# Bringing the rows of adaptive modulation into columns: transposes and a VectorE reduce instead of picking products

## The chip, the cores and the metric

The kernel runs on one core of one Trainium2 chip, as one program with one launch. The metric is the device time of the program in microseconds (us). Five engines work side by side, each through its own list of instructions in order, and wait for each other by semaphores: TensorE (PE, with its weight loads PEld), VectorE (DVE), ScalarE (ACT), GpSimd (POOL), and SyncE (SP), which here only issues loads. SBUF is the memory on the chip; PSUM holds TensorE's results, in eight banks of 512 fp32 columns.

## What is computed

Three transformer layers for 256 latent and 256 context tokens of width 1024. The first block has gated DeltaNet, a short convolution and a Fourier mix, and a SwiGLU feed-forward layer; the second block has a layer of retention and mLSTM and a layer of windowed attention, each with its feed-forward layer. Every layer takes its shifts, scales and gates from two condition vectors, one for the latent tokens and one for the context. That part is what the change touches:

```python
mod = jax.nn.silu(c) @ w_mod[layer] + b_mod[layer]
sh1, sc1, g1, sh2, sc2, g2 = jnp.split(mod[:, None, :], 6, axis=-1)
mod_c = jax.nn.silu(c_ctx) @ w_mod[layer] + b_mod[layer]
csh1, csc1, cg1, csh2, csc2, cg2 = jnp.split(mod_c, 6)
...
def modulate(t, gain, shift, scale):
    return rmsnorm(t, gain) * (1 + scale) + shift
```

w_mod is 1024 by 6144 for each of the three layers: 75 MB in fp32 of the 258 MB that the kernel reads.

## The kernel before

Activations lie with features on partitions and tokens on the free dimension. All large products split their fp32 weights in two parts: ScalarE writes wh (line 1517), VectorE or GpSimd writes wl = raw - wh (lines 2037 and 751), and TensorE adds three products (lines 855 to 857, 872 to 874 and 969 to 971). Weights come in 1 MB chunks through three buffers named raw; SyncE issues the next load when the chunk three before it has been used.

The order is a plan written out by hand (`make_plan`): it numbers every PSUM tile in the order in which TensorE fills it. A tile takes the bank of its number modulo eight, so TensorE, at `begin`, waits until the tile eight before it has been read out and freed (`free`, semaphore `bank_free`). `full` waits for a filled tile, `evacuated` for a freed one. `link` is used where an instruction reads what the one before it on its own engine wrote: it adds to the engine's own semaphore and waits for it.

**A modulation chunk** is 256 of the 6144 columns of one layer; there are 24 a layer, 72 in all, numbered 0 to 71. `mod` on TensorE does two things at each call. First the *row* of chunk n (line 906): eight products of 32 columns of condition vectors with 256 columns of weights. The k-th product goes to the 32 partitions of quadrant k % 4, so the result stands in four partial sums: partitions 32j and 32j+1 hold partial j for the latent and for the context vector. The other 30 partitions of a quadrant hold products of neighbouring columns, which nobody uses. ScalarE copies the 128 by 256 result to `modrow` (line 1527, two buffers). Then the *pick* of chunk n - 1 (line 914): `modrow`, 128 columns at a time, is the stationary operand, and the constant `pick`, 128 by 2 with a one in rows 32j of column 0 and rows 32j+1 of column 1, the moving one. That brings features onto partitions and adds the four partial sums: 128 by 2 for each half, 4 columns in the tile `modcol`. VectorE adds the bias and writes `mods` (line 2054), and after chunks 7 and 19 of a layer makes `coef` from the scales (line 2062), which the norms read.

The plan puts nine chunks at the start (the first norm waits for eight of them), six between the first projection's tiles, sixteen into the four steps s of the DeltaNet scan, four around the output projections, and the others into the norms, the feed-forward layers, the retention, the mLSTM and the attention. In the norm stages the order on TensorE is: spread of the reciprocal root (line 946), row, pick, row; ScalarE copies the second row before it writes h_hi (line 1558), and VectorE writes h_lo (line 2095) before TensorE goes on.

In a step of the scan TensorE's order is GR, KK, then row and pick of two chunks, the transpose of a mask product (X0T, line 1098), row and pick, the second X0T, row and pick, and the loop over levels, which begins with line 1112. VectorE takes X0T out of PSUM (line 2280), then does its four chunks in a row (`mod(4)`), then in the last two steps eight operations of line 2290, and then waits for the level loop (line 2328). GpSimd multiplies masks beside it (line 772), with both operands in SBUF. The tile `modcol` of the fourth chunk is eight tiles behind that of the first, so its pick waits until VectorE has finished the first.

Of the kernel before, what the change touches and what calls it, by code (L numbers as in the profile page):

```python
# [30 lines left out]
ALU = mybir.AluOpType  # L31
ACT = mybir.ActivationFunctionType
AX = mybir.AxisListType

P = 128
# [366 lines left out]
def build(nc, dram, out):  # L402
# [26 lines left out]
    modrow = sb("modrow", [P, 2, 256])  # L429
    mods = sb("mods", [P, 3, 48, 2])  # L430
# [17 lines left out]
    def S(name):  # L448
        a, b = SMALL[name]
        return small[:, a:b]  # L450
# [9 lines left out]
    ident = CA("ident")  # L460
# [143 lines left out]
    def bank(*key):  # L604
        return ps[:, tile[key] % BANKS, :]

    def free(ins, *key):
        ins.then_inc(bank_free[tile[key] % BANKS], 1)
# [210 lines left out]
    def _(pe):  # L819
# [74 lines left out]
        def mod_one():  # L894
            n = modn[0]
            modn[0] += 1
            if n == 0:
                pe.wait_ge(sem("cst_ready"), 1)
            if n < MODS:
                w = slot("mod", n)  # L900
                b = begin("modrow", n)

                for k in range(KD):
                    j = k % 4
                    o = SMALL["cvec"][0] + 16 * min(n // 24, 1) + 2 * k
                    ins = nc.tensor.matmul(b[32 * j:32 * j + 32, 0:256], small[:, o:o + 32],  # L906
                                           w[:, 256 * k:256 * k + 256], start=(k < 4), stop=(k >= 4),
                                           skip_group_check=True)
                close(ins)
            if 0 < n <= MODS:  # L910
                evacuated(pe, "modrow", n - 1)
                b = begin("modcol", n - 1)
                for i in range(2):
                    ins = nc.tensor.matmul(b[:, 2 * i:2 * i + 2], modrow[:, (n - 1) % 2, P * i:P * i + P], S("pick"),  # L914
                                           start=True, stop=True)
                close(ins)

        def mod(count=1):
# [97 lines left out]
        m = 0  # L1016
# [11 lines left out]
        b = begin("gt", 0)  # L1028
# [999 lines left out]
    def _(dve):  # L2028
# [14 lines left out]
        def mod(count=1):  # L2043

            for _ in range(count):
                n = modn[0]
                modn[0] += 1
                if 0 < n <= MODS:
# [2 lines left out]
                    lay, c = n // 24, n % 24  # L2051
                    o = 48 * lay + 2 * c
                    bias = S("bmod")[:, o:o + 2].unsqueeze(2).to_broadcast([P, 2, 2])
                    free(V.tensor_tensor(mods[:, lay, 2 * c:2 * c + 2, :],
                                         bank("modcol", n)[:, 0:4].rearrange("p (m v) -> p m v", m=2), bias,
                                         ALU.add), "modcol", n)
                    if c in (7, 19):
                        evacuated(dve, "modcol", n)
# [883 lines left out]
```

## Time and profile before

| | us |
|---|---|
| median of 3 runs | 1952.01 |
| lowest and highest | 1947.19, 1953.04 |
| profiled execution | 1949.81 |
| its span, first to last instruction | 1948.0 |

| engine | busy us | share of the span |
|---|---|---|
| TensorE | 1802.1 | 93% |
| TensorE weight loads | 1553.2 | 80% |
| VectorE | 909.6 | 47% |
| ScalarE | 763.3 | 39% |
| GpSimd | 477.1 | 24% |

The mean granted clock of TensorE was 0.962 of full speed; the clock has two levels, 1.0 (2.4 GHz) and 0.5 (1.2 GHz). A busy share is a mean over stages with different limits, so it says which engine is worth looking at, not what an instruction less is worth. For that the chain of work that ended last is read: it goes back from the last instruction, at each step to what released it.

### The profile page before, as it was taken

The numbers are of one execution on the slowest core, as the hardware profiler recorded it, in microseconds if no ns is written. First come the engines' busy times: TensorE is split into PE (matmuls) and PEld (weight loads), VectorE is DVE, ScalarE is ACT, GpSimd is POOL, SyncE is SP. The second block draws the span as 40 slices with busy tenths as digits, with TensorE's granted clock in tenths as the row PEclk, the third lists the DMA queues.
The fourth block names the chain that finished last, engine by engine and source line by source line (L and its number), as shares of the span: only waits on it lengthen the run. The fifth ranks groups of instructions, "written<-read, shape, count | busy, mean of one in ns | idle before, by whom it ended". The sixth has DMA issues, their size and how long they took to land.

```text
span 1948.0 us, 34252 instructions
## 1 busy us (share of the span) xinstructions
PE 1802.1 (93%) x14608; PEld 1553.2 (80%) x14608; DVE 909.6 (47%) x1659; ACT 763.3 (39%) x1330; POOL 477.1 (24%) x240
## 2 busy tenths in 40 slices
PE   5998998988799999998979789999999989999999
PEld 3777897877789999787778567888888767579998
DVE  1648626565344333535586744222231347744343
ACT  3454532233335564421544324222222344655443
POOL 0135322121113433111233011211212211013443
PEclk8999999999899999899989889999999999999999
DMA  8443244232264544323111123323222337034543
GB/s 316 174 162 130 89 172 153 89 110 88 109 253 163 190 178 168 136 69 127 54 65 66 68 85 130 131 107 130 109 108 103 114 123 274 27 144 162 193 175 129
DMA packets 36581, 261.58 MB, mean 134 GB/s; under 512 B 4048, under 2 KB 4176, under 8 KB 6224
## 3 DMA queue, kind: packets, MB, share of 16 engines
q1 hardware_dynamic: 36432, 259.40, 36.2%
q8 instruction: 117, 1.92, 0.4%
q14 instruction: 32, 0.26, 0.0%
HBM read 258.34 MB, written 1.05 MB: 133 GB/s over the span
## 4 chain that ended last, share of the span: by engine, by line
PE 79%; DVE 11%; ACT 4%; issue 3%; DMA 2%; POOL 1%; SPq 0%; DVEq 0%; ACTq 0%
PE ps L855 19%; PE ps L856 18%; PE ps L857 18%; PE ps L882 2%; PE ps L906 2%; PE ps L969 1%; PE ps L872 1%; PE ps L1124 1%; PE ps L873 1%; PE ps L874 1%; PE ps L970 1%; DVE msq L2492 1%; PE ps L971 1%; PE ps L1112 1%; PE ps L1475 1%
## 5 line engine op out<-in xcount | busy, mean ns | idle before, releaser
L751 POOL TENSOR_TENSOR wl<-raw,wh 128x1024 fp32r<-128x1024 f32 (+1 forms) x179 | 426.5, 2385 | 1241.4 <-ACT wh L1517 1241.4
L855 PE MATMUL ps<-h_hi,wh 128*128 128x256 f32 (+1 forms) x1696 | 556.7, 328 | 5.4 <-POOL wl L751 3.9
L856 PE MATMUL ps<-h_lo,wh 128*128 128x256 f32 (+1 forms) x1696 | 548.9, 324 | 0.0
L857 PE MATMUL ps<-h_hi,wl 128*128 128x256 f32 (+1 forms) x1696 | 548.9, 324 | 0.0
L1517 ACT ACTIVATE wh<-raw 128x1024 fp32r<-128x1024 f32 (+1 forms) x330 | 342.2, 1040 | 402.9 <-PE ps L857 287.5
L855 PEld LDWEIGHTS ps<-h_hi,wh 128*128 128x128 f32 x1696 | 327.8, 193 | 34.3 <-POOL wl L751 7.8
L856 PEld LDWEIGHTS ps<-h_lo,wh 128*128 128x128 f32 x1696 | 327.6, 193 | 25.8 <-issue 2.4
L857 PEld LDWEIGHTS ps<-h_hi,wl 128*128 128x128 f32 x1696 | 327.3, 193 | 23.8
L2037 DVE TENSOR_TENSOR wl<-raw,wh 128x1024 fp32r<-128x1024 f32 (+1 forms) x151 | 187.6, 1242 | 244.3 <-ACT wh L1517 233.1
L855 PE MATMUL ps<-gh,wh 128*128 128x256 f32 (+1 forms) x528 | 169.2, 320 | 0.0
L856 PE MATMUL ps<-gl,wh 128*128 128x256 f32 (+1 forms) x528 | 168.1, 318 | 0.0
L857 PE MATMUL ps<-gh,wl 128*128 128x256 f32 (+1 forms) x528 | 168.1, 318 | 0.0
L2116 DVE TENSOR_TENSOR sil<-ps,sil 128x256 f32<-128x256 f32 (+1 forms) x66 | 33.9, 513 | 258.6 <-PE ps L857 257.2
L855 PEld LDWEIGHTS ps<-gh,wh 128*128 128x128 f32 x528 | 100.5, 190 | 8.7 <-issue 2.0
L857 PEld LDWEIGHTS ps<-gh,wl 128*128 128x128 f32 x528 | 100.6, 190 | 6.9
L856 PEld LDWEIGHTS ps<-gl,wh 128*128 128x128 f32 x528 | 100.6, 191 | 6.8
L1596 ACT ACTIVATE sil<-ps 128x256 f32<-128x256 f32 (+1 forms) x66 | 30.0, 455 | 162.2 <-PE ps L857 160.5
L906 PE MATMUL ps<-raw,small 128*32 128x256 f32 x1152 | 85.5, 419 | 4.0 <-DMA raw<-in_mod 3.5
L1527 ACT ACTIVATE modrow<-ps 128x256 f32<-128x256 f32 x72 | 26.9, 381 | 125.3 <-PE ps L906 125.2
L914 PEld LDWEIGHTS ps<-small,modrow 128*128 128x128 f32 x288 | 40.3, 202 | 40.4 <-issue 30.1
L772 POOL TENSOR_TENSOR d_Xc<-d_Ac,const 128x256 f32<-128x256 f32 x40 | 31.6, 808 | 155.7 <-DVE d_Ac L2271 132.4
L872 PE MATMUL ps<-wh,h_hi 128*128 128x256 f32 x160 | 49.5, 310 | 17.5 <-POOL wl L751 11.0
(417 smaller groups left out, 2694.3 us busy)
## 6 DMA issues: line engine op xcount, KB each, us to landing
raw<-in_mod SPq DMA_DIRECT2D x72, 1024.0 KB, 5.0
raw<-in_ffn_in SPq DMA_DIRECT2D x66, 1024.0 KB, 4.8
raw<-in_ffn_out SPq DMA_DIRECT2D x24, 1024.0 KB, 4.8
raw<-in_w_in SPq DMA_DIRECT2D x16, 1024.0 KB, 4.8
raw<-in_w_gate SPq DMA_DIRECT2D x12, 1024.0 KB, 4.9
raw<-in_w_ab SPq DMA_DIRECT2D x12, 1024.0 KB, 4.8
raw<-in_ffn_out SPq DMA_DIRECT2D x12, 768.0 KB, 4.3
raw<-in_w_at SPq DMA_DIRECT2D x5, 1024.0 KB, 4.9
```

The lines of the kernel that those rows point to most:

```text
L751: nc.gpsimd.tensor_tensor(wl[e % SPLIT][:, 0:entries[e]["words"]], part(e), wh[e % SPLIT][:, 0:entries[e]["words"]].bitcast(F32), ALU.subt ...
L772: nc.gpsimd.tensor_tensor(Xc[:, d, lv % 2], Ac[:, d], mask.unsqueeze(1).to_broadcast([P, 4, 64]), ALU.mult).then_inc(sem("x_level"), 1)
L855: nc.tensor.matmul(b[:, cols], wh[e % SPLIT][:, w], xh(k), start=(k == 0), stop=False)
L856: nc.tensor.matmul(b[:, cols], wh[e % SPLIT][:, w], xl(k), start=False, stop=False)
L857: ins = nc.tensor.matmul(b[:, cols], wl[e % SPLIT][:, w], xh(k), start=False, stop=(k == nk - 1))
L872: nc.tensor.matmul(b[:, 0:256], h_hi[:, k, tk], wh[e % SPLIT][:, w], start=(k == 0), stop=False)
L882: ins = nc.tensor.matmul(b[:, 0:cols], w(k), rhs(k), start=(k == 0), stop=(k == nk - 1))
L906: ins = nc.tensor.matmul(b[32 * j:32 * j + 32, 0:256], small[:, o:o + 32], w[:, 256 * k:256 * k + 256], start=(k < 4), stop=(k >= 4), skip ...
L914: ins = nc.tensor.matmul(b[:, 2 * i:2 * i + 2], modrow[:, (n - 1) % 2, P * i:P * i + P], S("pick"), start=True, stop=True)
L1517: A(wh[e % SPLIT][:, 0:x["words"]], part(e), ACT.Copy).then_inc(hi_ready, 1)
L2037: V.tensor_tensor(wl[e % SPLIT][:, 0:entries[e]["words"]], part(e), wh[e % SPLIT][:, 0:entries[e]["words"]].bitcast(F32), ALU.subtract).th ...
L2116: free(V.tensor_tensor(sil[:, j % 4, c0:T], bank("fb" + nm, j)[:, c0:T], sil[:, j % 4, c0:T], ALU.mult), "fb" + nm, j)
```

## The change

The pick of a chunk becomes two transposes: `modrow`, 128 columns at a time, stays the stationary operand, and the identity is the moving one in transpose mode. The tile `modcol` then holds 256 columns instead of 4: for each half m the four quadrants j of 32 columns, of which the first two (r = 0 and 1) are the partial sums of the two vectors. VectorE's one instruction becomes two: a reduce over j out of PSUM into `mods`, linked, and an addition of the bias on `mods` in place, which frees the tile. Each pick keeps its place on TensorE. In the changed kernel the lines between 914 and 2054 have numbers smaller by one.

```diff
                 evacuated(pe, "modrow", n - 1)
                 b = begin("modcol", n - 1)
                 for i in range(2):
-                    ins = nc.tensor.matmul(b[:, 2 * i:2 * i + 2], modrow[:, (n - 1) % 2, P * i:P * i + P], S("pick"),
-                                           start=True, stop=True)
+                    ins = nc.tensor.transpose(b[:, P * i:P * i + P], modrow[:, (n - 1) % 2, P * i:P * i + P], ident)
                 close(ins)
...
                     bias = S("bmod")[:, o:o + 2].unsqueeze(2).to_broadcast([P, 2, 2])
-                    free(V.tensor_tensor(mods[:, lay, 2 * c:2 * c + 2, :],
-                                         bank("modcol", n)[:, 0:4].rearrange("p (m v) -> p m v", m=2), bias,
+                    parts = bank("modcol", n)[:, 0:256].rearrange("p (m j r) -> p m r j", m=2, j=4)[:, :, 0:2, :]
+                    link(V.tensor_reduce(mods[:, lay, 2 * c:2 * c + 2, :], parts, AX.X, ALU.add))
+                    free(V.tensor_tensor(mods[:, lay, 2 * c:2 * c + 2, :], mods[:, lay, 2 * c:2 * c + 2, :], bias,
                                          ALU.add), "modcol", n)
                     if c in (7, 19):
                         evacuated(dve, "modcol", n)
```

VectorE in the second step of the scan, before the change; d_TTc is the last work on X0T, d_TTc and d_Tmc behind it belong to the level loop:

```order
209 L2280 TENSOR_TENSOR d_TTc<-const_60,ps 128x256 x2
210 L2054 TENSOR_TENSOR mods<-ps,small 128x4 x2
211 L2062 SCALAR_TENSOR_TENSOR coef<-mods,small 128x16
212 L2054 TENSOR_TENSOR mods<-ps,small 128x4 x2
213 L2328 TENSOR_TENSOR d_TTc<-d_TTc,ps 128x256
```

The same place after it:

```order
237 L2280 TENSOR_TENSOR d_TTc<-const_60,ps 128x256 x2
238 L2054 TENSOR_REDUCE mods<-ps 128x4
239 L2055 TENSOR_TENSOR mods<-mods,small 128x4
240 L2054 TENSOR_REDUCE mods<-ps 128x4
241 L2055 TENSOR_TENSOR mods<-mods,small 128x4
242 L2062 SCALAR_TENSOR_TENSOR coef<-mods,small 128x16
243 L2054 TENSOR_REDUCE mods<-ps 128x4
244 L2055 TENSOR_TENSOR mods<-mods,small 128x4
245 L2054 TENSOR_REDUCE mods<-ps 128x4
246 L2055 TENSOR_TENSOR mods<-mods,small 128x4
247 L2328 TENSOR_TENSOR d_TTc<-d_TTc,ps 128x256
```

Each addition out of PSUM (ps) has become a reduce out of PSUM and an addition with both operands in SBUF (mods and the bias in small). VectorE behind the mLSTM, before the change, where rml is the low half of the output projection's input:

```order
741 L2495 TENSOR_TENSOR mout<-mout,gb 128x512
742 L2054 TENSOR_TENSOR mods<-ps,small 128x4 x2
743 L2641 TENSOR_TENSOR rml<-rout,rmh 128x512 x4
744 L2641 TENSOR_TENSOR rml<-mout,rmh 128x512 x4
745 L2037 TENSOR_TENSOR wl_55<-raw_49,wh_52 128x1024
```

And after it:

```order
809 L2495 TENSOR_TENSOR mout<-mout,gb 128x512
810 L2054 TENSOR_REDUCE mods<-ps 128x4
811 L2055 TENSOR_TENSOR mods<-mods,small 128x4
812 L2054 TENSOR_REDUCE mods<-ps 128x4
813 L2055 TENSOR_TENSOR mods<-mods,small 128x4
814 L2641 TENSOR_TENSOR rml<-rout,rmh 128x512 x4
```

Four instructions stand in front of rml in place of two.

## Rows read from the trace of the kernel before

**Rows 1.** The page's part 4: shares of the chain that ended last, by engine.

```profile
PE 79%; DVE 11%; ACT 4%; issue 3%; DMA 2%; POOL 1%; SPq 0%; DVEq 0%; ACTq 0%
```

**Rows 2.** Lines 914 and 2054 by source: duration ns min/median/max, first and last start, form.

```profile
L914 PE MATMUL ps<-small,modrow x288: 165/251/374, 20.3 to 1770.0; 128*128 128x2 f32 x144
L2054 DVE TENSOR_TENSOR mods<-ps,small x72: 147/154/164, 21.0 to 1770.4; 128x4 f32<-128x4 f32 x72
```

**Rows 3.** Timeline, TensorE, chunk 8: start us, us, engine, line, operation, count.

```profile
62.98 0.61 PE L914 MATMUL ps<-small,modrow 128*128 128x2 f32 x4
63.45 0.48 PE L855 MATMUL ps<-h_hi,wh 128*128 128x512 f32 x1
```

**Rows 4.** Transposes of line 1058: by source, and timeline of TensorE at their end.

```profile
L1058 PE MATMUL ps<-const_all,qk x16: 272/272/273, 227.3 to 230.2; 128*128 128x128 f32 x16
...
230.36 0.60 PE L1058 MATMUL ps<-const_all,vT 128*128 128x128 f32 x4
230.71 0.36 PE L855 MATMUL ps<-h_hi,wh 128*128 128x256 f32 x1
```

**Rows 5.** The chain in order of time (start us, us, what), at chunks.

```profile
63.05 0.54 PE ps L914 x4
...
125.81 0.54 PE ps L914 x4
...
791.07 0.54 PE ps L914 x4
...
1220.41 0.54 PE ps L914 x4
...
1513.33 0.54 PE ps L914 x4
```

**Rows 6.** The chain at chunk 6, and the timeline of transposes at the lower clock.

```profile
38.03 0.94 PE ps L914 x4
...
1657.12 1.97 PE L1475 MATMUL ps<-const_all,sc 128*128 128x128 f32 x8
```

**Rows 7.** Timeline of GpSimd, VectorE and TensorE in the scan's second step.

```profile
363.29 2.33 POOL L772 TENSOR_TENSOR d_Xc<-d_Ac,const 128x256 f32<-128x256 f32 x3 [2.03 <-DVE d_Ac L2271]
...
364.50 0.47 DVE L2062 SCALAR_TENSOR_TENSOR coef<-mods,small 128x16 f32<-128x16 f32 x1
365.00 0.32 DVE L2054 TENSOR_TENSOR mods<-ps,small 128x4 f32<-128x4 f32 x2
...
364.54 0.58 PE L914 MATMUL ps<-small,modrow 128*128 128x2 f32 x4 [0.22 <-DVE mods L2054]
```

**Rows 8.** Lines 2535 and 2062 by source: duration ns min/median/max.

```profile
L2535 DVE TENSOR_TENSOR tiny<-scr,rM x8: 147/149/2399, 1017.2 to 1029.4; 32x1 f32<-32x1 f32 x8
...
L2062 DVE SCALAR_TENSOR_TENSOR coef<-mods,small x6: 174/174/470, 43.8 to 1655.4; 128x16 f32<-128x16 f32 x6
```

**Rows 9.** Timeline of GpSimd and TensorE at the output projection's third tile.

```profile
552.36 2.41 POOL L751 TENSOR_TENSOR wl<-raw,wh 128x1024 fp32r<-128x1024 f32 x1 [30.56 <-ACT wh L1517]
...
555.12 0.28 PE L855 MATMUL ps<-mgh,wh 128*128 128x256 f32 x1
```

**Rows 10.** Timeline at two splits and their use, and the chain at chunks 63 and 67.

```profile
1125.98 0.77 PE L855 MATMUL ps<-rmh,wh 128*128 128x512 f32 x1 [6.72 <-DVE rml L2641]
...
1195.71 1.22 DVE L2037 TENSOR_TENSOR wl<-raw,wh 128x1024 fp32r<-128x1024 f32 x1
...
1197.48 0.39 PE L855 MATMUL ps<-h_hi,wh 128*128 128x512 f32 x1
...
1644.70 0.15 DVE mods L2054
...
1654.34 0.84 PE ps L914 x4
```

**Rows 11.** Windows: length; busy PE, PEld, DVE, ACT, POOL; granted clock; DMA share, GB/s.

```profile
227.30:230.70 3.40, 3.40 (x33) 3.40 (x32) 0.00 (x0) 3.15 (x7) 0.00 (x0) 1.00 0.00 0
26.30:43.30 17.00, 15.70 (x107) 9.00 (x108) 0.70 (x5) 2.01 (x6) 0.00 (x0) 0.50 0.93 367
```

## The prediction, made before the changed kernel ran

> **What bounds the kernel now.** Read the chain of work that ended last first: TensorE holds 79% of the span, VectorE 11% [rows 1]. So a TensorE instruction taken out pays only where the chain passes through it. Next read the two lines that the change replaces [rows 2]: line 914 has 288 records, four in each of 72 chunks, because one fp32 product leaves two records; line 2054 on VectorE has 72 of 0.15 us. Then read the chain stretch by stretch and note for every chunk whether its products stand in it. They do for chunks 8 to 13 (six pieces, first and last shown), for chunks 49 to 55 (seven, first and last shown), for 32 and 33, and for one chunk in each norm stage, where the order is spread, row, pick, row, then ScalarE's copy of that row [rows 5]. They don't for chunks 0 to 5, beside which the chain runs through loads, nor for most picks of the scan, of the retention and of the attention projections, where TensorE waits later for something else.
>
> **The price of one chunk on TensorE.** Four records of 2 columns start at 62.98 and the dense product behind them at 63.45: 0.47 us [rows 3]. Transposes of 128 by 128 in fp32 stand in this kernel already, at line 1058: one record each, 272 ns long, a group of four in 0.60 us, so (0.60 - 0.27) / 3 = 0.11 us a step; behind the last group, begun at 230.36, the next dense product starts at 230.71 [rows 4]. Two should hold the engine for 0.14 us by that row. A first transpose after other work takes some 0.05 us more, by the group at 1657.12 whose eight fill 1.97 us at the lower clock, so I take 0.20. The gain is **0.27 us a chunk**, with 0.15 (if most of the 0.47 is the changeover from the row) and 0.33 as ends. At 1.2 GHz the four take 0.94 us in the chain [rows 6]; two at (1.97 - 0.42) / 7 = 0.22 us a step take 0.44, so 0.5 less.
>
> **TensorE's gains, place by place.**
> - The head: only chunk 6 is in the chain, at the lower clock: 0.5 us.
> - Chunks 8 to 13: 6 x 0.27 = 1.6 us. TensorE has no gap there.
> - Chunks 32 and 33 would give 0.54, but GpSimd's split for the third tile of w_o ends at 552.36 + 2.41 = 554.77, and TensorE uses it at 555.12 [rows 9]: 0.35 us, the rest turns into a wait.
> - One chunk in each of the four norm stages (37, 47, 57, 69) and one after the mLSTM (42): 5 x 0.27 = 1.35 us.
> - Chunks 49 to 55: 7 x 0.27 = 1.9 us.
> - Chunks 66 and 67 in front of the softmax, the second at the lower clock with 0.84 us in the chain [rows 10]: 0.27 + 0.4 = 0.7 us. Chunk 71: 0.15 us.
> - Chunks 59 to 64: nothing. The chain there runs through loads, splits and VectorE, and TensorE's records are not in it.
>
> Together 6.55 us, out of some 19 us (72 x 0.27) that the engine is relieved of.
>
> **VectorE's costs.** The trace has no reduce of this size. The nearest rows are the 128x4 add out of PSUM, 0.15 us [rows 2], and the 128x16 operation of line 2062, 0.17 us without a wait [rows 8]; from those I take 0.16, between 0.15 and 0.25 for sixteen strided elements. It is linked: the instruction behind it waits on VectorE's own semaphore. After the linked line 2062, which ends at 364.97, the next starts at 365.00 [rows 7], so 0.03 more. The add behind it takes the place of the old one. So **0.19 us a chunk** of VectorE time, 0.18 to 0.28. It counts where VectorE is the chain:
> - Chunks 44 and 45 stand straight before the split of line 2641, for which TensorE waits until 1125.98 [rows 10]: 2 x 0.19 = 0.4 us.
> - Chunks 63 and 64 stand in VectorE's rotation of the last queries, in the chain at 1644.70 [rows 10]: 0.4 us.
> - In ffn, the reduce starts earlier by what TensorE saves, so nothing; in front of the first ffn tile after a norm, three chunks add 0.57 us, against a split that ends at 1195.71 + 1.22 = 1196.93 and is used at 1197.48, 0.55 us later [rows 10]: nothing, or 0.1.
>
> **The added wait that matters.** The old add had one operand in PSUM. The new one reads mods and bmod, both in SBUF. Look at what happens to such instructions beside a GpSimd tensor operation: line 2535, one column on 32 partitions, takes 149 ns as a rule and 2399 at worst, and line 2062, which also reads two SBUF operands, 174 and at worst 470 [rows 8]. That 470 stands in the scan at 364.50, while GpSimd's masks ran from 363.29 for 2.33 us; the two adds out of PSUM at 365.00, beside the same masks, took 0.32 us together and were not held [rows 7]. So the new add will be held until the running mask operation ends. Of the 72 adds the sixteen of the scan lie beside GpSimd's masks; the few others that meet a GpSimd operation stand where nobody waits for VectorE. In the scan the last pick needs the bank that the first of VectorE's four chunks frees: the trace has that wait, 0.22 us [rows 7]. Queued behind this pick on TensorE is line 1112, the first product of the level loop. With the change the first add ends at about 364.97 instead of 364.40, the pick starts 0.57 later and is 0.27 shorter: line 1112 starts 0.3 us later. Three of the scan's four steps: 0.9 us lost. In the first step nothing waited for the bank; two shorter picks and the held add give about 0.15 back. **Net cost in the scan 0.75 us**, between a gain of 0.6 if the add isn't held and a loss of 4. The upper end: with all four adds held one by one, VectorE leaves the four chunks up to 1.7 us late in the last two steps, of which I count 0.7 us as slack before the level loop's second round.
>
> **The sum.** 6.55 - 0.75 - 0.4 - 0.4 = **5.0 us less**. The profiled execution took 1949.8 us around a span of 1948.0; the sum gives 1944.8. The median of the three runs shown is 1952.0, 2.2 above it, so the forecast is **1947.0 us**, a quarter of a per cent. A measurement of this kernel can tell about 0.3%, 5.9 us, from no change.
>
> **Rivals.**
> 1. *No hold in the scan and cheap changeovers.* If the lock doesn't bite, the scan gives 0.6 instead of costing 0.75, and at 0.30 a chunk the rest gains 0.6: 7 us less, 1945. For it: the 0.14 us row. Against: the 470 ns at just this place. Chance 0.20.
> 2. *The gain is given back.* At 0.15 us a chunk the TensorE sum is 3.9, and with a reduce of 0.25, the held adds on the path and the splits late by 0.1 the costs reach 3: 1 us less, 1951. Against: the dense stream shows no other reason for its 0.47 us. Chance 0.20.
> 3. *The clock: slower than before.* TensorE's granted clock was 0.50 from 26.30 to 43.30, behind a wait for loads [rows 11], and line 914 takes 0.94 us in place of 0.47 there. If transposes in place of products let the clock fall more often in the chunk stretches, each further microsecond at 1.2 GHz on dense products costs half of itself. The kernel would be slower from 10 us of additional low clock on, and 0.3% slower from 22 us. Price at 24 us: 12 - 5 = 7 us more, 1959. Against: line 1058's stretch, nothing but transposes, shows a clock of 1.00 [rows 11]. Chance 0.05.
>    The Trainium skill, "TensorE: Matmul & The Clock Gate", Part 4: PE-mode transpose, says that transpose mode does not count as a busy TensorE and that the higher clock doesn't engage for it. By that rule line 1058's stretch should have fallen; its row doesn't show it, over 3.4 us, so I leave the sum as it is.
> 4. *The change doesn't do what it says.* If a transpose by these operands left two records as the products do, nothing would be gained, and 1.5 us of costs would stay: 1953.5. Against: line 1058 has 16 records for 16 transposes [rows 4]. Chance 0.05.
>
> **How the numbers follow.** The forecast has 0.50, with its own range 1944.5 to 1949.5. The range over the cases: from 1943, below rival 1 by the scatter of the runs, to 1953, above rival 2; rival 3 and half of rival 4 stay out. Faster by over 0.3%: a quarter of the forecast and three quarters of rival 1, 0.12 + 0.15 = 0.27. Slower by over 0.3%: rival 3 and a little of 4, 0.06. Within: 0.67.
>
> **What would show it.** Right: line 914 with 144 records of some 272 ns; next dense product 0.20 us behind a chunk's first transpose; reduces of 0.16 us; in the scan's last three steps the add at 0.5 us or more and line 1112 about 0.3 us later behind GpSimd's masks; TensorE's busy time down by 15 to 20 us and its waits up by most of that. Wrong: transposes at two records, adds of 2.4 us in the ffn, more than 10 us of additional low clock, or GpSimd's splits moving so that a chunk meets them where none does now.

## The result

The changed kernel took 1934.2 us, the median of six executions (1930.6 to 1937.5), the kernel before 1952.5 in the six beside them (1947.2 to 1958.4). The ratio is 0.9915, 95% interval 0.9894 to 0.9935. Two later comparisons gave 0.9921 (0.9908 to 0.9934) and 0.992 (0.990 to 0.994). So the change makes the kernel faster by 14 to 18 us. I had forecast 5 us, and 1934 lies below the whole of my range of 1943 to 1953.

The profiled execution took 1934.65 us around a span of 1932.6, which is 15.4 less than the 1948.0 of before.

First the lines that answer to [rows 1, 2]: the page's part 4, and lines 914, 2054 and the new 2055 by source (instructions, then the shortest, median and longest in ns, first and last start, form). The lines between these places have moved up by one: L855 and L906 are the same, L1112 of before is L1111.

```profile
PE 78%; DVE 12%; ACT 4%; issue 3%; DMA 1%; POOL 1%; SPq 0%; DVEq 0%; ACTq 0%
...
L914 PE MATMUL ps<-const_all,modrow x144: 270/314/476, 19.7 to 1754.7; 128*128 128x128 f32 x144
...
L2054 DVE TENSOR_REDUCE mods<-ps x72: 159/168/176, 20.1 to 1755.2; 128x4 f32<-128x16 f32 x72
...
L2055 DVE TENSOR_TENSOR mods<-mods,small x72: 161/163/2214, 20.3 to 1755.4; 128x4 f32<-128x4 f32 x72
```

The 288 records have become 144. The reduction takes 0.17 us, near the 0.16 that I took. The new add takes 0.16 and is held up to 2.2 us.

Chunk 8, which answers to [rows 3], and chunk 57 in a norm stage, where another chunk's row stands behind the transposes; timeline of TensorE (start us, us, engine, line, operation, count):

```profile
61.40 0.44 PE L914 MATMUL ps<-const_all,modrow 128*128 128x128 f32 x2
61.59 0.48 PE L855 MATMUL ps<-h_hi,wh 128*128 128x512 f32 x1
...
1553.75 0.44 PE L914 MATMUL ps<-const_all,modrow 128*128 128x128 f32 x2
1554.11 1.07 PE L906 MATMUL ps<-raw,small 128*32 128x256 f32 x16
```

In front of a dense product the chunk's end takes 61.59 - 61.40 = 0.19 us, where it took 0.47: 0.28 saved, as forecast. In front of a row it takes 0.36. There the four products of before took 0.53 (1566.93 to 1567.46 below), so only 0.17 is saved.

```profile
1566.93 0.61 PE L914 MATMUL ps<-small,modrow 128*128 128x2 f32 x4
1567.46 1.07 PE L906 MATMUL ps<-raw,small 128*32 128x256 f32 x16
```

Chunks 8, 13, 49 and 55 in the chain after the change, which answer to [rows 5]:

```profile
61.47 0.37 PE ps L914 x2
...
122.87 0.37 PE ps L914 x2
...
1209.14 0.37 PE ps L914 x2
...
1500.41 0.37 PE ps L914 x2
```

From chunk 8 to chunk 13 it is now 61.40 us, where it was 125.81 - 63.05 = 62.76; from chunk 49 to chunk 55 it is 291.27, where it was 1513.33 - 1220.41 = 292.92. In these two stretches the clock was 1.00 in both kernels. So each chunk there gives back its 0.27 us on the path, and no more.

What I had left out shows in the granted clock. Here is part 1's and part 2's line of TensorE, first of before, then of after (busy time; then the granted clock in tenths of full speed in 40 slices of the span):

```profile
PE 1802.1 (93%) x14608; PEld 1553.2 (80%) x14608; DVE 909.6 (47%) x1659; ACT 763.3 (39%) x1330; POOL 477.1 (24%) x240
...
PEclk8999999999899999899989889999999999999999
```

```profile
PE 1773.3 (92%) x14464; PEld 1517.5 (79%) x14464; DVE 925.9 (48%) x1731; ACT 763.0 (39%) x1330; POOL 477.3 (25%) x240
...
PEclk8999999999899999999989899999999999999999
```

TensorE's busy time fell by 28.8 us. By my price without the clock, 72 x 0.27 = 19 was the most to be expected. The mean clock rose from 0.962 to 0.969 in the two profiled executions. The clearest place is the first ffn's start, 10 us around the same work in each kernel. The view is that of windows: length, then busy time of PE, PEld, DVE, ACT and POOL, then granted clock, DMA share and GB/s. Before, then after:

```profile
579.00:589.00 10.00, 9.30 (x51) 7.75 (x52) 6.98 (x21) 5.29 (x11) 0.00 (x0) 0.51 0.52 197
```

```profile
570.00:580.00 10.00, 7.76 (x66) 6.75 (x67) 7.89 (x22) 5.64 (x11) 0.00 (x0) 1.00 0.62 226
```

At a clock of 0.51 the engine is busy for 9.3 us with 51 records. At 1.00 it does 66 in 7.8. Added over the span, the profile of before has 147 us at 1.2 GHz, with TensorE busy in 123 of them. The profile of after has 119 us, busy in 89.

### The profile page after: what moved, and what is told of

It reads as the page before. It is cut to its first block, busy times and chain, and to the rows that moved or that the text cites. A ratio compares the mean times of both kernels' runs of the same rounds, so it can differ in the third digit from the quotient of the medians.

```text
span 1932.6 us, 34036 instructions
## 1 busy us (share of the span) xinstructions
PE 1773.3 (92%) x14464; PEld 1517.5 (79%) x14464; DVE 925.9 (48%) x1731; ACT 763.0 (39%) x1330; POOL 477.3 (25%) x240
## 4 chain that ended last, share of the span: by engine, by line
PE 78%; DVE 12%; ACT 4%; issue 3%; DMA 2%; POOL 1%; SPq 0%; DVEq 0%; ACTq 0%
PE ps L855 19%; PE ps L856 18%; PE ps L857 18%; PE ps L882 2%; PE ps L906 2%; PE ps L872 1%; DVE msq L2492 1%; PE ps L873 1%; PE ps L874 1%; PE ps L1123 1%; PE ps L1111 1%; PE ps L1129 1%; PE ps L1474 1%; ACT wh L1516 1%; PE ps L928 1%
## 5 line engine op out<-in xcount | busy, mean ns | idle before, releaser
L855 PE MATMUL ps<-h_hi,wh 128*128 128x256 f32 (+1 forms) x1696 | 555.4, 327 | 7.7 <-POOL wl L751 5.2
L855 PEld LDWEIGHTS ps<-h_hi,wh 128*128 128x128 f32 x1696 | 325.9, 192 | 38.2 <-POOL wl L751 10.0
L855 PE MATMUL ps<-gh,wh 128*128 128x256 f32 (+1 forms) x528 | 169.2, 320 | 0.0
L855 PEld LDWEIGHTS ps<-gh,wh 128*128 128x128 f32 x528 | 100.6, 190 | 8.7 <-issue 2.0
L906 PE MATMUL ps<-raw,small 128*32 128x256 f32 x1152 | 83.8, 412 | 8.1 <-DMA raw<-in_mod 5.4
L872 PE MATMUL ps<-wh,h_hi 128*128 128x256 f32 x160 | 48.3, 302 | 17.5 <-POOL wl L751 10.9
L906 PEld LDWEIGHTS ps<-raw,small 128*32 128x32 f32 x1152 | 32.9, 115 | 39.7 <-issue 19.8
```

Of the source, the lines that this page charges most:

```text
L855: nc.tensor.matmul(b[:, cols], wh[e % SPLIT][:, w], xh(k), start=(k == 0), stop=False)
L872: nc.tensor.matmul(b[:, 0:256], h_hi[:, k, tk], wh[e % SPLIT][:, w], start=(k == 0), stop=False)
```

## The experiments

Two theories. **T**: time saved on TensorE's path made the gain, at more places than I had counted. **C**: the other way of moving the columns keeps TensorE's clock at 2.4 GHz more of the time. A third, **L**, is that the profiled execution was lucky with its clock. VectorE's cost was to be measured by itself. Each kernel ran beside the kernel before on the same chip. The ratio and its 95% interval are taken over the executions of both; "us" is the difference of the two medians, and an interval in us is that of the ratio times the median of before. "Clock" is the mean of the granted clocks of the kernel's executions.

| kernel | columns through TensorE in a chunk's end | ratio to before | 95% interval | us | clock |
|---|---|---|---|---|---|
| before | 4 x 2 | 1 | | | 0.960 |
| half_pick | 2 x 2 | 0.9956 | 0.9940 to 0.9972 | -9.1 | 0.960 |
| wide_pick32 | 4 x 32 | 0.9977 | 0.9967 to 0.9987 | -5.3 | 0.963 |
| half_wide | 2 x 128 | 0.9922 | 0.9905 to 0.9939 | -15.4 | 0.970 |
| the changed kernel, again | 2 x 128 | 0.9921 | 0.9908 to 0.9934 | -16.7 | 0.971 |
| the changed kernel, a third time | 2 x 128 | 0.9920 | 0.9900 to 0.9940 | -13.7 | 0.971 |
| four_tr | 4 x 128 | 0.9955 | 0.9943 to 0.9968 | -8.6 | 0.973 |
| wide_pick | 4 x 128 | 0.9940 | 0.9926 to 0.9954 | -10.9 | 0.975 |
| dve_only | 4 x 2 | 1.0014 | 1.0005 to 1.0024 | +2.2 | 0.958 |
| head_tr | 2 x 128 in 8 chunks | 0.9995 | 0.9981 to 1.0008 | -0.8 | 0.963 |
| scan_tr | 2 x 128 in 20 chunks | 0.9998 | 0.9987 to 1.0009 | +0.2 | 0.963 |
| batch_add | 2 x 128 | 0.9921 | 0.9907 to 0.9935 | -14.6 | 0.971 |
| batch_add_2, the same once more | 2 x 128 | 0.9924 | 0.9907 to 0.9941 | -14.3 | 0.970 |
| mix_scan | 2 x 128, 4 x 128 in 24 | 0.9921 | 0.9907 to 0.9935 | -16.5 | 0.971 |
| mix_head_scan | 2 x 128, 4 x 128 in 32 | 0.9910 | 0.9896 to 0.9924 | -18.3 | 0.973 |
| batch_head | 2 x 128, 4 x 128 in 8 | 0.9931 | 0.9915 to 0.9948 | -13.4 | 0.972 |
| before_fill | 4 x 2, fills in waits | 0.9974 | 0.9956 to 0.9992 | -6.1 | 0.973 |
| after_fill | 2 x 128, fills in waits | 0.9942 | 0.9926 to 0.9957 | -12.1 | 0.982 |
| after_fill2 | the same, longer fills | 0.9908 | 0.9893 to 0.9923 | -16.7 | 0.985 |

**The yardstick.** The changed kernel, on the chip of the next three.

> The changed kernel unchanged, as the yardstick of this chip. Every theory expects a ratio near 0.9915 to the kernel before, thus 16 to 18 us less. Theory C (the low-clock time of this kernel is shorter because TensorE spends the chunk's end otherwise) expects a mean granted clock of about 0.970 in each of its runs against about 0.962 before; theory L (the low-clock windows fell luckily in the profiled execution) expects the mean clock to scatter from run to run as much as the two kernels differ.

Its six executions had clocks from 0.969 to 0.973, the 20 of before beside them from 0.958 to 0.964. They don't overlap, so L falls: the higher clock belongs to the kernel.

**Nearly the same time, but transposes.**

```diff
-                for i in range(2):
+                for i in (0, 1, 0, 1):
                     ins = nc.tensor.transpose(b[:, P * i:P * i + P], modrow[:, (n - 1) % 2, P * i:P * i + P], ident)
```

> The changed kernel with each of a chunk's two transposes issued twice: four TensorE instructions a chunk, as before, so that TensorE's time for a chunk's end is nearly what the four products took (about 0.45 us), while the columns go through as transposes and VectorE reduces and adds. Theory T (the gain is time saved on TensorE's path, directly or by what it shifts) expects about the time of before plus VectorE's link, 0 to 2 us over it: ratio 1.000 to 1.001. Theory C (transposes of 128 columns keep the clock up where products with 2 columns did not) expects the clock part of the gain to stay, some 10 of the 17 us: ratio 0.994 to 0.996, mean clock near 0.970.

Measured: 0.9955, clock 0.973. A chunk's end takes 0.41 us in front of a dense product (59.01 to 59.42), against 0.47 before. With the instruction count of before and VectorE's longer link, 8.6 us are gained, and the clock is as high as the changed kernel's or higher. T in its pure form, which wanted 1.000, is out.

**Less time, and fewer columns.**

```diff
-                for i in range(2):
+                for i in range(1):
                     ins = nc.tensor.matmul(b[:, 2 * i:2 * i + 2], modrow[:, (n - 1) % 2, P * i:P * i + P], S("pick"),
                                            start=True, stop=True)
...
-                                         bank("modcol", n)[:, 0:4].rearrange("p (m v) -> p m v", m=2), bias,
+                                         bank("modcol", n)[:, 0:2].unsqueeze(1).to_broadcast([P, 2, 2]), bias,
```

> The kernel before with two of a chunk's four picking products left out (the second half's columns are not computed and the first half's are added in their place): TensorE saves about 0.2 us a chunk without a transpose and without a longer link on VectorE. Theory T by my forecast's sum expects 4 to 6 us less, ratio 0.997 to 0.998, and if a saving on the path is multiplied by the clock's windows, up to 0.992. Theory C expects only the path's 4 to 6 us, and the mean clock as before, 0.962.

Measured: 0.9956, clock 0.960 as before. Its chunk end takes 0.24 us in front of a dense product (chunk 8, 62.90 to 63.15), 0.23 less than before. Time saved pays too, by 9.1 us (5.5 to 11.7), at an unchanged mean clock: its profile has 152 us at 1.2 GHz, busy in 122, as before. At 0.23 us a chunk my places come to 6.55 x 0.23 / 0.27 = 5.6 us, at the low end of that interval. This kernel's range was wide, from 1931 us at a clock of 0.966 to 1948 at 0.953. In the ten microseconds at the first ffn it still fell to the lower clock:

```profile
576.00:586.00 10.00, 8.87 (x50) 7.32 (x49) 6.98 (x21) 5.63 (x11) 0.28 (x1) 0.51 0.48 193
```

**VectorE's part alone.**

```diff
-                    free(V.tensor_tensor(mods[:, lay, 2 * c:2 * c + 2, :],
-                                         bank("modcol", n)[:, 0:4].rearrange("p (m v) -> p m v", m=2), bias,
+                    parts = bank("modcol", n)[:, 0:4].rearrange("p (m v j) -> p m v j", m=2, j=1)
+                    link(V.tensor_reduce(mods[:, lay, 2 * c:2 * c + 2, :], parts, AX.X, ALU.add))
+                    free(V.tensor_tensor(mods[:, lay, 2 * c:2 * c + 2, :], mods[:, lay, 2 * c:2 * c + 2, :], bias,
                                          ALU.add), "modcol", n)
```

> The kernel before with one more VectorE instruction a chunk between its picking products and the add of the bias (a reduction over one term each): the longer link on VectorE alone, nothing changed on TensorE. My forecast's sum expects 1 to 2 us more (0.4 at chunks 44 and 45, 0.4 at 63 and 64, 0.75 in the scan): ratio 1.0005 to 1.001. If a later release in the scan lets the following work come in a better order, as the gain of some 5 us in the scan's stretch of the changed kernel could mean, it expects less time than before: ratio 0.997.

Measured: 1.0014, 2.2 us more (by the interval 1.0 to 4.7). My sum had 0.4 + 0.4 + 0.75, and without the shorter picks 0.9 in place of 0.75: 1.7. The term is right within the interval. But the clock of its executions was 0.958, against 0.961 in those of before beside them, so a part of the 2.2 us may be the clock's; the run can't part the two. The idea that a later release in the scan helps is out.

**Columns alone.** This separates the two halves of C: is it the transpose, or how much the engine moves?

```diff
-                    ins = nc.tensor.matmul(b[:, 2 * i:2 * i + 2], modrow[:, (n - 1) % 2, P * i:P * i + P], S("pick"),
-                                           start=True, stop=True)
+                    ins = nc.tensor.matmul(b[:, P * i:P * i + P], modrow[:, (n - 1) % 2, P * i:P * i + P],
+                                           S("pick").unsqueeze(1).to_broadcast([P, 64, 2]), start=True, stop=True)
...
-                                         bank("modcol", n)[:, 0:4].rearrange("p (m v) -> p m v", m=2), bias,
+                                         bank("modcol", n)[:, 0:256].rearrange("p (m r) -> p m r", m=2)[:, :, 0:2], bias,
```

> The kernel before with the two picking products of a chunk given 128 moving columns (the same two columns 64 times over) in place of 2; four TensorE instructions a chunk as before, VectorE as before. Theory C1 (what the chunk's end puts through TensorE in columns is what moves the clock) expects the mean clock of the transposing kernels, 0.970 to 0.975, against 0.960 before; the instructions themselves get longer (from 0.11 us to perhaps 0.19 to 0.22 us each, thus up to 0.35 us a chunk in a row), so the time itself may stand anywhere from 1940 to 1955. Theory C2 (something else of a transpose does it, not its columns) expects the clock to stay at 0.960 and the time at 1950 to 1960.

Timeline of TensorE at chunk 8 and at chunk 57, and windows of the first ffn's start, in this kernel:

```profile
60.02 0.71 PE L914 MATMUL ps<-small,modrow 128*128 128x128 f32 x4
60.49 0.48 PE L855 MATMUL ps<-h_hi,wh 128*128 128x512 f32 x1
...
1557.82 0.71 PE L914 MATMUL ps<-small,modrow 128*128 128x128 f32 x4
1558.46 1.07 PE L906 MATMUL ps<-raw,small 128*32 128x256 f32 x16
```

```profile
572.00:582.00 10.00, 8.25 (x71) 7.10 (x70) 7.52 (x19) 5.61 (x12) 0.00 (x0) 1.00 0.65 241
```

In front of a dense product the chunk's end takes 60.49 - 60.02 = 0.47 us, what it took with 2 columns [rows 3]. In front of a row it takes 1558.46 - 1557.82 = 0.64, which is 0.11 more than the 0.53 of before. No instruction is gone, VectorE does the same addition, and the kernel is 10.9 us faster (9.0 to 14.4). The clock was 0.974 to 0.977 in its six executions, against 0.957 to 0.963 in the 23 of before beside them. The stretch that fell to 0.51 before stands at 1.00, and the whole profile has 97 us at 1.2 GHz, TensorE busy in 73, where before had 147 and 123. This is the strongest single piece of evidence: 10.9 us can be had with no transpose and no time saved at the chunk's end. That they come by way of the clock is read from these profiles; no run sets the clock by itself. My guess that these instructions would take up to 0.35 us more a chunk was too high: it is nothing in front of a dense product and 0.11 in front of a row.

**One size between.** The diff is against wide_pick.

```diff
-                    ins = nc.tensor.matmul(b[:, P * i:P * i + P], modrow[:, (n - 1) % 2, P * i:P * i + P],
-                                           S("pick").unsqueeze(1).to_broadcast([P, 64, 2]), start=True, stop=True)
+                    ins = nc.tensor.matmul(b[:, P * i:P * i + 32], modrow[:, (n - 1) % 2, P * i:P * i + P],
+                                           S("pick").unsqueeze(1).to_broadcast([P, 16, 2]), start=True, stop=True)
```

> As the kernel with the picking products widened to 128 moving columns, but to 32 columns: only this size is changed. If the clock follows the columns in steps, the mean clock lies between 0.961 (2 columns) and 0.975 (128 columns), and the time between 1937.5 and 1948.5 us. If 2 columns are special in another way, it equals the 128 columns, 0.975 and 1937.5.

Measured: clock 0.963 and 5.3 us less, between 2 and 128 columns in both. 2 columns are not special.

**Both, without transposes and without the link.** half_pick's edit, with 128 columns in its one product.

> The two changes of the chunk's end that the transposes combine, without a transpose and without VectorE's longer link: one product (two TensorE instructions) a chunk with 128 moving columns, the second half's columns left out and the first half's added in their place. Apart, the columns gave 10.9 us and the two instructions fewer 9.1 us. If the two add up, 20 us less than before, ratio 0.990 (1928 to 1929 us), and the changed kernel, which has both and VectorE's link, is 2 to 4 us above it by that link. If they overlap, as time saved moves what the clock sees, 1931 to 1934 us, the changed kernel's own time, and the link costs nothing.

Measured: 15.4 us less, which lies between what the two readings expected and near the overlapping one. The changed kernel, with VectorE's link on top, had 13.7 to 18.3 us less on three other occasions. So the two gains overlap: columns gave 10.9 us alone and 15.4 - 9.1 = 6.3 on top of the saved time; the saved time gave 9.1 alone and 15.4 - 10.9 = 4.5 on top of the columns. One reason may be this, by the table: two instructions less also take half the columns away, and the clock of the kernels with 2 x 128 is 0.970 to 0.971, of those with 4 x 128 it is 0.973 to 0.975.

**Where?** Transposes in the first eight chunks alone, or in the scan's 20 alone; in both kernels the other chunks keep the picking products (`if 0 <= n - 1 < 8` and `if 14 <= n - 1 < 34` around the two forms).

> Transposes and the reduction for the first eight chunks alone (up to 60 us), the picking products for the other 64. The trace of the changed kernel was 1.6 us ahead of the one before at the first projection, and the kernel with four transposes a chunk some 4 us ahead at the same place. Expected: 1 to 5 us less than before, ratio 0.9975 to 0.9995, mean clock 0.961 to 0.964. If these chunks were the main place of the gain it would be 0.993.

> Transposes and the reduction for chunks 14 to 33 alone, the scan's (from 310 to 545 us), the picking products for the others. The trace of the changed kernel gained 5.5 us in this stretch where my forecast's sum lost 0.75. The forecast's term expects 0 to 1 us more than before; the reading of the traces expects 4 to 7 us less: ratio 0.9965 to 0.998, with less low clock between 310 and 545 us than the 44 us of before.

Neither differs measurably from before. (The 44 us in the second expectation is a slip: the profile of before has 30.7 us of low clock between 310 and 545 us, and so has that of scan_tr.) The expectation of 4 to 7 us in the scan failed. The gain of 5.5 us that the changed kernel's trace shows in that stretch was not due to the scan's own transposes alone. Both clocks, 0.963, are a little above before's. I can't name one place of the gain. The other 44 chunks, those of the first projection, the ffns, the retention, the mLSTM and the attention, were not tried alone: the gain may lie with them, or need all 72.

**VectorE's add inside the changed kernel.** The reduction frees the tile, and the bias is added once for four chunks.

```diff
-                    link(V.tensor_reduce(mods[:, lay, 2 * c:2 * c + 2, :], parts, AX.X, ALU.add))
-                    free(V.tensor_tensor(mods[:, lay, 2 * c:2 * c + 2, :], mods[:, lay, 2 * c:2 * c + 2, :], bias,
-                                         ALU.add), "modcol", n)
+                    free(V.tensor_reduce(mods[:, lay, 2 * c:2 * c + 2, :], parts, AX.X, ALU.add), "modcol", n)
+                    if c % 4 == 3:
+                        evacuated(dve, "modcol", n)
+                        part4 = mods[:, lay, 2 * c - 6:2 * c + 2, :]
+                        bias = S("bmod")[:, o - 6:o + 2].unsqueeze(2).to_broadcast([P, 8, 2])
+                        link(V.tensor_tensor(part4, part4, bias, ALU.add))
                     if c in (7, 19):
-                        evacuated(dve, "modcol", n)
```

> The changed kernel with the reduction freeing the tile and the bias added once for four chunks (18 additions in place of 72): this takes the second VectorE instruction, which GpSimd held in the scan, off the way between the reduction and the next product. The picks with VectorE's longer link alone cost 2.2 to 2.7 us more than before. If the same cost sits in the changed kernel, this one is 2 to 3 us below it: ratio to before 0.990 to 0.991 (1929 to 1930 us). If TensorE's clock takes it back, it equals the changed kernel, 0.992.

The scan's second step in the changed kernel, timeline of all engines, which answers to [rows 7]:

```profile
358.98 2.34 POOL L772 TENSOR_TENSOR d_Xc<-d_Ac,const 128x256 f32<-128x256 f32 x3 [2.03 <-DVE d_Ac L2271]
...
359.93 0.17 DVE L2054 TENSOR_REDUCE mods<-ps 128x4 f32<-128x16 f32 x1
...
360.13 0.52 DVE L2055 TENSOR_TENSOR mods<-mods,small 128x4 f32<-128x4 f32 x1
...
360.80 0.41 PE L914 MATMUL ps<-const_all,modrow 128*128 128x128 f32 x2 [0.79 <-DVE mods L2055]
...
361.14 0.74 PE L1111 MATMUL ps<-d_TTc,d_Xc 64*64 64x64 f32 x18
```

The same place with the batched add:

```profile
359.92 0.24 DVE L2054 TENSOR_REDUCE mods<-ps 128x4 f32<-128x16 f32 x2
...
360.23 0.41 PE L914 MATMUL ps<-const_all,modrow 128*128 128x128 f32 x2 [0.23 <-DVE mods L2054]
...
360.57 1.15 PE L1111 MATMUL ps<-d_TTc,d_Xc 64*64 64x64 f32 x32
```

The hold is there as forecast: the add that takes 0.16 elsewhere takes 0.52 beside GpSimd's masks, and the pick waits 0.79 in place of 0.22. Both kernels have their step's first pick at 352.04. The level loop's first product starts 9.10 us after it in the changed kernel and 8.53 with the batched add. In the kernel before it was 8.69, with the picks at 356.36 and 364.54:

```profile
356.36 0.61 PE L914 MATMUL ps<-small,modrow 128*128 128x2 f32 x4
...
365.05 1.15 PE L1112 MATMUL ps<-d_TTc,d_Xc 64*64 64x64 f32 x32
```

Yet batch_add as a whole took 1933.8 us, a ratio of 0.9921, and that is the changed kernel's: of the two outcomes that I had named it is the second. On one chip with the changed kernel:

> The changed kernel once more, on the same chip as the two below, so that differences of 0.15% can be read. Expected 0.992 of before, mean clock 0.970 to 0.972.

> The changed kernel with the bias added once for four chunks. In the profiles a step of the scan fell by it from 9.09 to 8.53 us, three times, thus about 2 us less on the path in the scan. If what is saved in place stays, 2 us below the changed kernel on this chip; if the clock's windows take it back, within 1 us of it.

1934.7 and 1934.1 us, with intervals of the ratio that are 0.004 wide. Three steps at 0.57 would be 1.7 us; this measurement can neither show nor exclude it.

**Can both be had?** Wide products where VectorE's link is waited for, transposes elsewhere (first kernel); the first eight chunks by wide products too (second); that head with the batched add (third).

> A version that may beat both: transposes as in the changed kernel, but picking products with 128 moving columns and VectorE's single addition at the 24 chunks where VectorE's link is waited for (14 to 33 in the scan, 44, 45, 63 and 64). By the forecast's terms this gives back 0.75 in the scan and 0.8 at the four others, and keeps the columns: 1 to 3 us below the changed kernel, 0.990 to 0.9915 of before (1929 to 1932 us), mean clock 0.972 to 0.974. If the time saved in the scan counts, it is 0 to 4 us above the changed kernel.

> The same with the first eight chunks by wide picking products as well. In the traces the kernels with four TensorE instructions of 128 columns a chunk had 10 to 14 us of low clock in the first 60 us, the changed kernel 14 to 20 us. Expected against the version with the scan's chunks alone: 0 to 3 us less; if the rows' own time counts more than the clock there, 0 to 2 us more.

> The same, with the first eight chunks by picking products of 128 moving columns (four TensorE instructions each) and one addition, since the kernels with such heads had the least low clock. Expected 0 to 3 us below the batched addition alone (ratio to before 0.989 to 0.991), clock 0.972 to 0.975; if the added instructions of the head weigh more than its clock, 0 to 2 us above it.

0.9921, 0.9910 and 0.9931, all with the changed kernel's 0.9915 to 0.9921 inside their intervals. None beats it measurably.

**Fills in TensorE's waits.** If it is what TensorE does that moves its clock, then idle waits can be filled. Ahead of 19 waits the kernel transposes the identity into a bank that the next product overwrites, 4 to 46 times, 358 records in all. In some places the wait for the bank now stands ahead of the wait for data, with the fill between them:

```diff
+        def fill(b, key):
+            for _ in range(FILL.get(key, 0)):
+                nc.tensor.transpose(b[:, 0:P], ident, ident)
...
             b = begin(*key)
+            fill(b, key)
             for k in range(nk):
```

> The kernel before with its chunks untouched, and transposes of the identity (128 moving columns each, results overwritten) put ahead of 19 waits of TensorE of 0.8 to 8.7 us, each filled to about half. No work is saved or moved, so a gain can only come from the clock. Theory C (columns through TensorE are what moves the clock, and this made 12 of the 16 us): mean clock above the 0.960 of before, 0.970 to 0.985, and 6 to 20 us less; by the scatter of 60 runs of the kernel before, 0.01 of clock goes with 11.6 us. Theory T (time saved on the path made the gain, the clock only goes with it): clock and time as before, or 1 to 3 us more where a fill overshoots its wait.

> The changed kernel with the same fills. Theory C: the clock rises over its 0.971 (to 0.98 or more) and the time falls by 3 to 12 us below the changed kernel, ratio to before 0.985 to 0.990, which beats both kernels. Theory T: ratio 0.992 to 0.994.

> The changed kernel with the fills half as long again, about three quarters of each wait at the full clock, more than the whole wait at the low one. Theory C: a clock as high or higher than with the shorter fills, and a time within 3 us of theirs, later where a fill overshoots.

Windows of the stretch in which TensorE waits for the squares of the mLSTM's output and then for their splits, the same work in the kernel before (30 us long) and with the fills (27 us):

```profile
1105.00:1135.00 30.00, 15.50 (x51) 9.32 (x52) 23.74 (x24) 9.34 (x17) 0.00 (x0) 0.66 0.19 70
```

```profile
1093.00:1120.00 27.00, 19.33 (x125) 14.65 (x124) 23.75 (x23) 8.97 (x16) 0.00 (x0) 0.94 0.24 86
```

before_fill changes nothing at the chunks' ends and has a clock of 0.969 to 0.979 in place of 0.960. So the clock can be moved by work that is of no use, and the kernel is 6.1 us faster by it (1.6 to 8.6), at the low end of the 6 to 20 that C expected. That supports C in another place. But on top of the change C failed: after_fill has a clock of 0.982, 0.011 above the changed kernel's, and a ratio of 0.9942, where C wanted 0.985 to 0.990 and T 0.992 to 0.994. Longer fills, on the same chip, give 0.9908, again the changed kernel within the intervals. They are 4.6 us faster than the shorter ones by the medians, with intervals that don't overlap; I had expected them within 3 us, or later. So these runs show no cost of a longer fill, although in the trace of before_fill six of the 19 fills end with no wait left behind them (the one at 518.52 takes 6.91 us). Why the shorter fills gained less stays open. What is shown is that 0.011 to 0.014 of mean clock, had in waits, brought nothing measurable on top of the change.

**A price from scatter.** In 89 executions of the kernel before whose clock is on record, the clock lay between 0.955 and 0.964. The ten at 0.958 took 1952.6 us on average, the 25 at 0.960 took 1949.6, the 15 at 0.962 took 1947.3. A straight line through all of them has 11.7 us less for each 0.01 more (correlation -0.75). By that line the changed kernel's 0.011 is worth some 13 us, and 2 to 4 would be left for the path less VectorE. The line can't be carried to every kernel: before_fill's 0.013 would be 15 us, and was 6.

## Why the prediction was wrong, point by point

- **The price of a chunk, 0.27 us: right.** 0.28 in front of dense products, in the trace of after. On the path it is 0.27 at chunks 8 to 13 and 49 to 55, above. One kind of place was mis-sized: in front of another chunk's row (chunks 42, 47, 57, 66 and 69) it is 0.17. Of the 6.55 us of places that takes off 5 x 0.1 = 0.5. Chunks 37 and 67 changed their clock level between the two traces: 0.54 became 0.62 at the one, 0.84 became 0.37 at the other.
- **Records, reduction, link: right.** One record a transpose, 0.17 for the reduction, the add 0.20 behind its start (359.93 to 360.13), where I had 0.19. Rival 4 is out. dve_only puts the price of VectorE's longer link at 1.0 to 4.7 us, where the sum had 1.7.
- **The hold in the scan: right in kind, a little small.** Add 0.52 us, line 1111 later by 9.10 - 8.69 = 0.41 us a step in place of 0.3. So rival 1 is out. Nine of the scan's sixteen adds were held, not all (514 to 587 ns). Two adds of 2.2 us stand beside GpSimd's splits, one of them at the first ffn (580.24); "adds of 2.4 us in the ffn" was one of my signs of being wrong. The view of waits shows none for them.
- **The head** gave 1.6 us by the first projection (62.98 against 61.40) where I had 0.5. Part of that is the clock: at chunk 5 it was 0.50 before (34.51) and 1.00 after (32.49).
- **GpSimd's splits** take a part back, as I said for chunks 32 and 33: TensorE's waits for line 751 in the dense products rose from 3.9 us to 5.2. The view is that of waits (us in total, times, longest), before and after:

```profile
PE ps L855 <- POOL wl L751: 3.9, 5, 1.7
```

```profile
PE ps L855 <- POOL wl L751: 5.2, 6, 1.8
```

- **The net path gain of 5.0 us** can't be measured alone, but two things lie near it: the changed kernel's ratio of 0.9921 against the 0.9940 of the widened picks is 3.7 us, half_wide's 0.9922 against it 3.5 us; by the medians it is 5.8 and 4.5. That is an argument from differences between chips, each with some 2.5 us of uncertainty. half_pick, at an unchanged clock, gained 9.1 us where my terms come to 5.6, so the path term may be too small as well; its interval begins at 5.5.
- **The step that failed is the sum's treatment of the clock.** I worked out every term at the clock that its row had, and let the clock enter only as rival 3: a fall, slower, with a chance of 0.05. There was no case in which it rose; its gain stood in the sum at nothing, without a reason. But replacing four products of 2 columns by two transposes of 128 raised the mean clock by 0.011. Widening the products alone is worth 10.9 us (9.0 to 14.4 by the interval), and 6.3 on top of the saved time. So the missing term is some 6 to 11 us, as large as or larger than the whole 5.0 of the sum. I named "more than 10 us of additional low clock" as what would show me wrong; it was 28 us less. The trace of before had the hint: 147 us at the lower clock, and TensorE busy in 123 of them. I looked at [rows 11] only for what transposes might take away, and never asked what the picks themselves cost the clock.
- **A rule that I let stand.** By the Trainium skill, "TensorE: Matmul & The Clock Gate", Part 4: PE-mode transpose, transposes shouldn't count as a busy TensorE. Here four transposes of 128 columns a chunk gave 0.973 and four plain products of 128 columns 0.975, both far above the 0.960 of products with 2 columns. The fills, which are transposes and nothing else, raised before_fill's clock to 0.973. The measurement disagrees with that rule, and had I used it as a term, it would have pointed the wrong way.
- **The bounds.** My low end was the likeliest rival less the runs' scatter. An effect that I could only think of in one direction had no place in it.

What stays open: at which chunks the gain arises (those of head_tr and of scan_tr alone show none, the others were not tried alone), why wider products keep the clock up, and how the 9.1 us of half_pick split between its path and what its shorter stretches do to the clock. Its mean clock didn't rise, and its executions spread over 17 us.

## What to carry to other kernels

Before you price an edit on TensorE, add up how long its granted clock is at the lower level while the engine is busy; here it was 123 us, many times the 6.55 us that the edit was worth by its instructions. A product with very few moving columns may hold the engine nearly as long as one with 128: here four records took 0.47 us with either in front of a dense product, and 0.53 against 0.64 in front of a row. Widening them may keep the clock up, so try that small edit by itself first. Filling TensorE's waits raised the clock too, but gained 6.1 us on the kernel before and nothing measurable on top of the change. Measure the clock over several executions, not in one.

## What the runs showed of the hardware that I had not expected

- Two fp32 products with 128 by 128 weights hold TensorE for the same time with 2 and with 128 moving columns when a dense product stands behind them: their four records took 0.47 us to its start in both. In front of another chunk's row it was 0.53 and 0.64. Their own durations differ (medians 251 and 275 ns).
- The mean granted clock of one kernel scatters from execution to execution (0.955 to 0.964 in 89 of the kernel before, 0.974 to 0.977 in six of wide_pick, 0.953 to 0.966 in nine of half_pick), and the way in which 72 short chunk ends are done moves its mean: 0.960 with 4 x 2 or 2 x 2, 0.963 with 4 x 32, 0.970 to 0.971 with 2 x 128, 0.973 to 0.975 with 4 x 128.
- A VectorE add of 128x4 with both operands in SBUF took up to 2214 ns, where 163 is its median. That one stood beside a GpSimd operation of 2.35 us; beside GpSimd's masks of 0.7 us nine took 514 to 587 ns.
